# A feed-forward block on one core: join, convolution and gate work reordered on VectorE and ScalarE

## The reference

```python
u, v = jnp.split(hn @ w_ffn_in, 2, axis=-1)      # D_FF = 2816 each
up = jnp.pad(u, ((0, 0), (pad, pad), (0, 0)))
uc = conv_b
for t in range(CONV_W):
    uc = uc + up[:, t:t + L] * conv_w[t]
return (jax.nn.gelu(uc) * v).astype(dt) @ w_ffn_down
```

## Time and profile before

| quantity | value |
|---|---|
| median of 3 runs | 1283.27 us (1282.43 to 1284.66) |
| the profiled execution | 1282.7 us, its span 1280.9 us |
| PE busy | 1219.8 us, 95% |
| DVE busy | 875.3 us, 68% |
| ACT busy | 528.7 us, 41% |
| POOL busy | 195.6 us, 15% |
| mean granted TensorE clock | 0.986 |

### The profile page before, as it was taken

One profiled execution on the slowest core, in us unless ns is written; L12 is line 12 of the kernel. 1 busy time (PEld: TensorE's weight loads), 2 busy tenths in 40 slices (PEclk: granted clock), 3 DMA queues, 4 the chain that ended last, 5 costly groups with the idle time before them and its releaser, 6 DMA issues.

```text
span 1280.9 us, 18435 instructions
## 1 busy us (share of the span) xinstructions
PE 1219.8 (95%) x6989; PEld 1108.8 (87%) x6989; DVE 875.3 (68%) x1189; ACT 528.7 (41%) x832; POOL 195.6 (15%) x137
## 2 busy tenths in 40 slices
PE   6999999999999999999999979899899899899977
PEld 5999999999999988888888869789789789789965
DVE  7494585486377372232233799988998998898987
ACT  5353353335245152122221456535535535535544
POOL 0000000000000000000000314324324333433340
PEclk9999999999999999999999999999899899899989
DMA  4311111101201011111123012112121121121302
GB/s 168 134 35 49 68 44 50 61 33 49 78 33 49 34 54 62 66 62 69 65 94 131 22 66 80 53 68 81 50 77 72 50 83 66 50 82 67 115 17 99
DMA packets 23185, 86.14 MB, mean 67 GB/s; under 512 B 2512, under 2 KB 2768, under 8 KB 23120
## 3 DMA queue, kind: packets, MB, share of 16 engines
q1 hardware_dynamic: 22544, 83.90, 17.7%
q10 hardware_dynamic: 576, 1.38, 0.3%
HBM read 82.12 MB, written 3.15 MB: 67 GB/s over the span
## 4 chain that ended last, share of the span: by engine, by line
PE 83%; DVE 10%; issue 2%; DVEq 2%; ACT 1%; DMA 1%; POOL 0%; SPq 0%; ACTq 0%; POOLq 0%
PE ps L1507 43%; PE ps L1750 19%; PE ps L1833 10%; PE ps L1604 3%; PE ps L1544 3%; DVE ring L1232 2%; PE ps L1597 1%; PE ps L1614 1%; PE ps L1532 1%; DVE cb L1315 1%; DVE cb L1296 1%; DVEq L1301 1%; DVE af L1251 1%; PE ps L1534 1%; DVE h L1219 1%
## 5 line engine op out<-in xcount | busy, mean ns | idle before, releaser
L1507 PE MATMUL ps<-hn,ring 128*128 128x256 f32 (+1 forms) x2544 | 462.6, 337 | 0.3 <-DVE hn L921 0.3
L1507 PEld LDWEIGHTS ps<-hn,ring 128*128 128x128 f32 x2544 | 388.3, 191 | 46.7 <-issue 0.7
L1750 PE MATMUL ps<-af,ring 128*128 128x384 f32 x1848 | 334.0, 340 | 33.0 <-DVE v L1288 21.0
L1750 PEld LDWEIGHTS ps<-af,ring 128*128 128x128 f32 x1848 | 325.8, 191 | 40.3 <-DVE v L1288 22.3
L1833 PE MATMUL ps<-ring,gf 128*128 128x512 f32 x693 | 161.0, 394 | 7.1 <-DVE gf L1331 6.8
L892 DVE TENSOR_TENSOR ring<-raw,ring 128x1024 fp32r<-128x1024 f32 x68 | 83.1, 1224 | 119.2 <-ACT ring L476 114.8
L1833 PEld LDWEIGHTS ps<-ring,gf 128*128 128x128 f32 x693 | 132.0, 191 | 35.1 <-issue 7.8
L1232 DVE TENSOR_TENSOR ring<-raw,ring 128x512 fp32r<-128x512 f32 x164 | 127.5, 810 | 13.5 <-ACT ring L713 13.3
L713 ACT ACTIVATE ring<-raw 128x512 fp32r<-128x512 f32 x164 | 96.6, 621 | 53.2 <-DMA raw<-in_pairs 42.0
L1467 POOL TENSOR_TENSOR sums<-raw 128x512 f32<-128x512 f32 x1 | 1.3, 1283 | 707.0 <-DMA raw<-in_pairs 707.0
L525 ACT ACTIVATE sig<-ps 128x768 f32<-128x768 f32 x36 | 29.2, 812 | 179.9 <-PE ps L1507 179.9
(11 more groups left out here) (171 smaller groups left out, 1297.8 us busy)
## 6 DMA issues: line engine op xcount, KB each, us to landing
raw<-in_units SPq DMA_DIRECT2D x68, 512.0 KB, 3.4
raw<-in_pairs SPq DMA_DIRECT2D x66, 512.0 KB, 3.5
strips<-in_strips SPq DMA_DIRECT2D x4, 896.0 KB, 4.6
x_in<-in_x_s SPq DMA_DIRECT2D x4, 512.0 KB, 5.4
h<-in_x_s SPq DMA_DIRECT2D x1, 2048.0 KB, 8.0
y_s<-hw SPq DMA_DIRECT2D x4, 512.0 KB, 3.0
x_in<-in_x_p SPq DMA_DIRECT2D x2, 512.0 KB, 7.4
h<-in_x_p SPq DMA_DIRECT2D x1, 1024.0 KB, 10.4
```

What stands on the lines that cost most here:

```text
L1507: ins = pe.matmul(out, w if stationary_w else x, x if stationary_w else w, start=start and i == 0, stop=stop and i == 2)
L1750: ins = pe.matmul(ps[:, bank, 0:HALF], ring[:, p, a, k * P:(k + 1) * P], af[:, x, b, k, :], start=first and k == 0 and j == 0, stop=k == H ...
```

## The change

Nothing is added or taken away; instructions move in the queues of DVE and ACT.

- DVE in tile i: conv(i-1) goes ahead of join_first(i), and so ahead of join_last(i-1) as well. The four sums of an odd tile (`gate_sums`) are split off from `gate` and go behind join_third(i).
- DVE at the end of stages 0 to 3: conv(hi-1) and join_last(hi-1), now in this order, go behind the pieces of the first down product; the gate product goes behind the residual sums of the second down product (from the first), its low part behind those of the third.
- ACT at the end of stages 0 to 3: gelu(hi-1) goes behind the high parts of the first down product's pieces, `gate_hi` one product later.
- At the end of the last stage: the A11 form of tile 20 gets its high and low parts ahead of conv(21) and gelu(21), A12 and A22 of the last pair get their low parts ahead of the sums.

```diff
@@ ScalarE, end of a stage
                 hi_upto(PLACE[hi - 1, S4] + 6)
-                gelu(hi - 1)
                 if hi == NF:
                     gate_hi(NF - 2)
+                    gelu(hi - 1)
                     gate_hi(NF - 1)
                 for n, x in enumerate(DOWN[d]):
                     hi_upto(PLACE[down_pair(qs[-1]), x] + 6)
-                    if n == 1 and hi < NF:
+                    if n == 0 and hi < NF:
+                        gelu(hi - 1)
+                    if n == 2 and hi < NF:
                         gate_hi(hi - 1)
@@ VectorE, gate
                 dve.tensor_tensor(cb[:], cb[:], v2[:], ALU.mult).then_inc(g32_done, 1)
+
+            def gate_sums(i):
+
+                q = i // 2
                 dve.tensor_tensor(GATE[S3], ge[:, 0:HALF], ge[:, HALF:T], ALU.subtract).then_inc(gs_done, 1)
...
                 dve.tensor_tensor(GATE[S1], ge[:, HALF:T], GATE[A22], ALU.add).then_inc(gs_done, 1)
-                if i == NF - 1:
-                    gate_lo(i - 1)
...
-            def gate_lo(i):
+            def gate_lo(i, forms=None):
                 q = i // 2
-                for x in GATES[:1] if i % 2 == 0 else GATES[1:]:
+                for x in forms or (GATES[:1] if i % 2 == 0 else GATES[1:]):
@@ VectorE, tiles
                     lo_upto(PLACE[i, A12] + 5)
+                    if i > lo:
+                        conv(i - 1)
                     if i > 0:
                         join_first(i)
                     if i > lo:
                         lo_upto(PLACE[i - 1, S4] + 5)
                         join_last(i - 1)
-                        conv(i - 1)
...
                     if i > 0:
                         join_third(i)
+                    if i > lo and i % 2 == 0:
+                        gate_sums(i - 1)
                     if i > lo and i < NF - 1:
                         gate_lo(i - 1)
                 lo_upto(PLACE[hi - 1, A22] + 5)
                 lo_upto(PLACE[hi - 1, S4] + 5)
-                join_last(hi - 1)
-                conv(hi - 1)
                 if hi == NF:
+                    join_last(hi - 1)
+                    gate_lo(NF - 2)
+                    conv(hi - 1)
                     gate(NF - 1)
-                    gate_lo(NF - 1)
+                    gate_lo(NF - 1, GATES[1:3])
+                    gate_sums(NF - 1)
+                    gate_lo(NF - 1, GATES[3:])
                 for n, x in enumerate(DOWN[d]):
                     if hi < NF or n < 6:
                         lo_upto(PLACE[down_pair(qs[-1]), x] + 5)
                     if hi < NF:
+                        if n == 0:
+                            conv(hi - 1)
+                            join_last(hi - 1)
                         down_sums(d, hi, qs, x, range(3))
-                        if n == 0:
+                        if n == 1:
                             gate(hi - 1)
-                        elif n == 1:
+                        elif n == 2:
                             gate_lo(hi - 1)
                         continue
```

## The result

The changed kernel takes 1325.48 us (median of 4 runs, 1322.73 to 1326.93) against 1283.19 for the kernel before: ratio 1.0326, 95% interval [1.0306, 1.0345]. The forecast was 1309.5 with a range up to 1320: right in its sign and in the place of the loss, too small in its size. The rest of this document is about which term was too small.

What follows compares the result with a forecast made beforehand. TensorE, busy 95% of the span, was taken as the bound. In-stage waits 33.1 plus clock 1.7, less 6.0 at stage ends and 2.0 in the last stage, gave +26.8 on 1282.7: 1309.5 us, range 1279 to 1320.

Steps and rivals of the forecast that it cites:

- Part 1, waits: Inside a stage, the convolution ahead of the joins makes TensorE wait for the last join: 33.1 us.
- Part 1, clock: Low TensorE clock behind those in-stage waits: 1.7 us charged for tile 1, nothing for odd tiles, 8.5 as upper bound.
- low clock too: Rival: the odd tiles' idle of 4.5 us drops TensorE's clock as 5.24 does, +8.5, 1318 us; chance 0.18.
- the 1.0 of tile 21: In tile 21, 1.0 of the 1.4 us wait goes into an existing wait for ACT's copy, leaving 0.4.
- Parts 2 and 3, stage ends: Third join ahead of gated sums, convolution, last join and gate later: third down product 1.5 us earlier, four times, 6.0.
- The wait for centre: At a stage's end, the second down product waits some 2 us for the bank that ACT's centre frees.
- Part 4: Last stage: tile 20's A11 low half goes ahead, 27 more matmuls run instead of waiting; gain 2.0 us.
- The new wait for a piece: Last stage: TensorE waits until 1235.3 for A12's weight piece for the third pair, at low clock afterwards.
- 5.8 us fitted into 6.3: Bare chain from A22's end through centre, convolution and joins, 5.8 us, against TensorE's 6.3 us of A12, S4, S2.

Runs made afterwards that it cites:

- e3: Changed kernel plus 12 filler matmuls on TensorE ahead of S1 in tiles 3, 7, 11, 15 and 19: 1319.46 us, ratio 1.0273.
- e1: Changed kernel with the convolution put back behind the joins inside a stage: 1286.86 us, ratio 1.0027 to the kernel before.
- e7: Kernel before with only the third join put ahead of the gated sums: 1287.81 us, ratio 1.0040.
- e8: Kernel before with only the last stage's new order: 1281.41 us, ratio 0.9991.
- e2: Kernel before with only the convolution put ahead of the joins inside a stage: 1312.49 us, ratio 1.023.
- e5: Changed kernel with the weight differences cut to 8 columns, not computing the layer: 1257.15 us.
- e6: Kernel before with the weight differences cut to 8 columns, not computing the layer: 1243.75 us.
- e4: Changed kernel with the weight piece that releases POOL's burst moved behind the convolution and first join: 1316.59 us, ratio 1.0257.
- e11: Kernel of e7 plus 12 filler matmuls ahead of the third down product in stages 0 to 3: 1283.84 us, ratio 0.9998 to the kernel before.

## Why the prediction was right in sign and wrong in size

**Part 1, waits: right.** Forecast 33.1 us of new waits, with 1.0 taken off for ACT's copy behind tile 21; 34.3 came, and the wait for ACT's third copy stayed (3.7 in all where it was 3.9). By kind: even tiles 1.25 forecast, 1.07 measured (tile 18: 1.38); odd tiles 4.5, measured 4.31; tile 1 4.6, measured 4.5 (6.64 less 2.12); tiles 2 and 20 0.3, measured 1.42 and 1.08; tile 21 1.4, measured 1.41. Tiles 4, 8, 12 and 16: none, none. Only tiles 2 and 20 were off: there the convolution met more of the burst than I gave it.

**Part 1, clock: the step that failed.** "I charge nothing and keep 5 x 1.7 = 8.5 as the upper bound." The idle of 4.3 us dropped the clock in every odd tile, so the rival *low clock too* was the true case, and its price was too small as well: 1.7 was read from work behind a 5.24 us wait, where 12 matmuls took 3.8 us, while behind 4.31 the low level lasted some 5 us and cost 2.5 (e3). Tile 1's fall, which I did charge with 1.7, cost 2.5 too (84 matmuls in 17.39 us, 14.86 at full clock). Five times 2.5 is 12.5 of the 17.4 us that were missing. I had set the chance of that rival to 0.18 and its time to 1318; with 2.5 it would have been 1322, just under the lowest run. What is left of the 17.4 is in small terms: tile 1's clock (0.8), tiles 2 and 20 (1.9), the stage ends (2.1), the 1.0 of tile 21 and 0.85 ahead of the block.

**Parts 2 and 3, stage ends: the right waits, the gain too large, its clock term wrong.** The third join's wait went and the wait for the residual sums came, as said. The third product came 2.5 us earlier (17.1 behind A22 instead of 19.6), more than the 1.5 forecast; from the start of S4 to it it is 15.0 us, where I expected 16 and it was 12.0. But the wait of 4.45 ahead of it drops the clock too, where I had counted the old low clock as gained: from there to the next stage 22.1 us instead of 20.4. Net 1.0 instead of 1.5, 2.1 us too much over four stages. With the in-stage order of before (e1, e7) it is a loss. The wait for centre that I put at 2 us did not show: the first two down products ran through (940.59 and its like, 36 matmuls in 8.36 us). The low halves that release centre ended 8.6 us behind A22 (at 944.92), where I had kept the 10.4 of before.

**Part 4: right in the changed kernel, not shown by itself.** 2.0 forecast, 2.5 in the stretch from tile 21's A22 to the end. The new wait for a piece was to be 5.4 us (1229.9 to 1235.3); it is 4.13. e8, the part by itself, is 1 us faster, but its profile has no gain in the last stage.

**The interaction that I had inside the sum.** The working of the odd tiles took the third join's new place into its chain, so the sum held it; e2 shows it apart: 2.94 against 4.31, with a fall of the clock in three odd tiles instead of five. The whole costs 10 us more than the parts by themselves (42.3 against 28.9 and 3.2).

**The rule from the Trainium skill** ("SBUF — State Buffer", Who interferes with whom): a DVE operation with two SBUF inputs contends with a GpSimd operation that reads SBUF, one with at most one SBUF input does not. The traces agree: 5.26 us for four operations beside three of POOL's, 2.37 without, 0.54 to 0.56 for a join in either case, and 29 of 42 us gone in e5 and e6.

## What to carry to other kernels

Before an operation is moved ahead of a short one with a deadline, add up the whole chain from its own latest input, with the other engine's burst (here POOL's) at its worst moment, and compare with the work that the waiting engine has in between. Here 5.8 us fitted into 6.3 only on paper: with the burst the odd tiles waited 4.31 us, and 1.42 even without it. Price a wait on TensorE at its length plus what the clock gives up behind it, and look where that falls: where the waiting engine has slack behind it, a part is covered; where it has none, all of it counts. When one wait goes and the engine that fed it is still the fullest, look for the next thing due from that engine, and move what has no deadline behind it.

## What the runs showed of the hardware that was not expected

- The idle that precedes a fall of TensorE's clock can be short, and idles of the same length went both ways. The windows behind them have a clock of 0.63 behind 2.26 us in stage 2 of e3 and 1.00 behind 2.28 and 2.26 in its stages 1 and 3; 0.50 to 0.59 behind 2.94 in three tiles of e2 and 1.00 in two; 0.50 and 1.00 behind 3.09 in stages 2 and 1 of e8; 0.65 and 1.00 behind 3.25 in tiles 11 and 7 of e4. Behind 2.12 before tile 1 of the kernel before it was 1.00, behind 2.58 in e11 0.54. Behind the waits of 3.87 (e2), 4.31, 4.45 and 5.24 us it fell each time; the longest idle with the clock at 1.00 behind it was 3.41 us, ahead of the last down products in e1 and e4. Below 3.87, the length of the idle alone does not decide.
- Two programs with the same order of DVE and POOL work at a stage's end took 5.24 and 3.09 us of wait for the same join (the kernel before and e8). In stage 1 of e8 the gated product and the first sum took 0.95 and 0.55 us while POOL's first operation took 2.91; in the kernel before they took 2.05, 1.62 and 1.58. A difference of 2 us there is no evidence of a better order.
